# First halves' norms as steps inside the projection passes, a column-tiled sample memory attention, and the prompt's gates beside a pass

## What is computed

```python
for l in range(2):
    h_p, h_s = rmsnorm(y_p, norm_pre[l]), rmsnorm(y_s, norm_pre[l])
    mk_p, mv_p = mem_kv(mem_prompt, mem_norm[l], w_mem_kv[l])     # 256 memory tokens, 4 heads of 128
    mk_s, mv_s = cache_mem_k[l], cache_mem_v[l]                   # the samples' own, from a cache
    if l == 0:   # forgetting attention, 8 heads of 128
        q, k, v, lf, xq, gate = split_fox(h @ fox_w_in, fox_b_f)  # lf = log_sigmoid(f + b_f)
        mix_p = fox_prompt(q, k, v, lf)       # scores + cumsum(lf)_i - cumsum(lf)_j, causal softmax
        mix_s = fox_sample(...)               # against 2048 paged past keys and the new ones
    else:        # multi-scale causal pooling of u
        u, xq, gate = split_pool(h @ pool_w_in)
        mix = multiscale_pool(u, ...)
    y = y + rmsnorm(concat(mix, mem_attend(xq, mk, mv)) * silu(gate) @ w_out[l], norm_post[l])
```

## Time and profile before

| | |
|---|---|
| Three runs | 3638.39, 3642.01, 3642.56 us (median 3642.01) |
| Profiled execution | 3641.81 us, its span 3640.2 us |
| Mean granted clock of TensorE | 0.968 |
| Busy share: PE, PEld, DVE, ACT, POOL | 92%, 78%, 37%, 31%, 11% |
| DMA | 515.75 MB, mean 142 GB/s |

### The profile page before, as it was taken

One profiled execution on the slowest core, in us unless ns is written; L12 is line 12 of the kernel. 1 busy time (PEld: TensorE's weight loads), 2 busy tenths in 40 slices (PEclk: granted clock), 3 DMA queues, 4 the chain that ended last, 5 costly groups with the idle time before them and its releaser, 6 DMA issues. The chain is left out here.

```text
span 3640.2 us, 51875 instructions
## 1 busy us (share of the span) xinstructions
PE 3365.5 (92%) x19681; PEld 2844.2 (78%) x19681; DVE 1345.5 (37%) x2667; ACT 1133.0 (31%) x2210; POOL 397.2 (11%) x613
## 2 busy tenths in 40 slices
PE   5999899899999998959999998995999899996999
PEld 4999799777777766748888887884999778775887
DVE  3332313232222213535545554223222335565322
ACT  3122323122222223435556553112113344212211
POOL 1330000001111110112222220000000001121000
PEclk9999999999999999979999999997999999997999
DMA  3344333278889973332322305332332434565541
GB/s 117 115 149 137 123 95 119 79 227 281 275 290 294 291 226 116 124 107 79 92 80 88 102 27 189 110 98 68 111 118 94 130 100 135 178 189 179 164 122 52
DMA packets 409348, 515.75 MB, mean 142 GB/s; under 512 B 50791, under 2 KB 298088, under 8 KB 407551
## 3 DMA queue, kind: packets, MB, share of 16 engines
q1 hardware_dynamic: 386263, 444.74, 39.3%
q0 software_dynamic: 22848, 67.78, 5.8%
HBM read 388.57 MB, written 124.22 MB: 141 GB/s over the span
## 5 line engine op out<-in xcount | busy, mean ns | idle before, releaser
L459 ACT ACTIVATE z_st_p<-bank 128x352 f32<-128x352 f32 (+3 forms) x325 | 168.1, 518 | 786.6 <-PE bank L434 777.5
L1596 PE MATMUL bank<-w_hi_o,b_hi_o 128*128 128x512 f32 x816 | 319.5, 392 | 27.0 <-DVE w_lo_o L1655 27.0
L434 PE MATMUL bank<-h00hi,w_hi_p 128*128 128x352 f32 x984 | 323.4, 329 | 17.3 <-DVE w_lo_p L401 7.9
L1597 PE MATMUL bank<-w_hi_o,b_lo_o 128*128 128x512 f32 x816 | 318.9, 391 | 0.0
L1598 PE MATMUL bank<-w_lo_o,b_hi_o 128*128 128x512 f32 x816 | 318.9, 391 | 0.0
L434 PE MATMUL bank<-h00hi,w_lo_p 128*128 128x352 f32 x984 | 318.0, 323 | 0.0
L434 PE MATMUL bank<-h00lo,w_hi_p 128*128 128x352 f32 x984 | 317.8, 323 | 0.0
L434 PE MATMUL bank<-h01hi,w_hi_p 128*128 128x512 f32 x656 | 283.6, 432 | 13.8 <-DVE w_lo_p L401 11.5
L759 PE MATMUL bank<-pT_fa,v_fa 128*128 128x256 f32 (+1 forms) x1152 | 291.4, 373 | 1.7 <-DVE mix_fa L832 0.7
L399 DVE CAST w_hi_p<-w_raw_p 128x1024 fp32r<-128x1024 f32 (+1 forms) x130 | 92.6, 713 | 476.5 <-PE bank L434 418.7
L434 PE MATMUL bank<-h01hi,w_lo_p 128*128 128x512 f32 x656 | 259.3, 395 | 0.0
(11 more groups left out here) (318 smaller groups left out, 6966.3 us busy)
## 6 DMA issues: line engine op xcount, KB each, us to landing
k_raw_sf<-in_cache_fox_k SPq DMA_DIRECT2D x128, 512.0 KB, 4.6
v_raw_sf<-in_cache_fox_v POOLq DMA_DIRECT2D x128, 512.0 KB, 5.4
z<-z_st_p SPq DMA_DIRECT2D x112, 512.0 KB, 2.9
w_raw_p<-in_fox_w_in SPq DMA_DIRECT2D x80, 512.0 KB, 5.4
b_raw_o<-bT SPq DMA_DIRECT2D x32, 768.0 KB, 6.4
w_raw_p<-in_pool_w_in SPq DMA_DIRECT2D x48, 512.0 KB, 5.1
out<-tok_p SPq DMA_DIRECT2D x64, 256.0 KB, 3.2
w_raw_o<-in_w_out SPq DMA_DIRECT2D x24, 512.0 KB, 4.5
```

The source lines that it names most:

```text
L434: last = nc.tensor.matmul(bank[:, 0:width], wt[:, u, k, :], h[:, k, at0:at0 + width], start=(m == 0), stop=(m == MM - 1))
L459: nc.scalar.activation(z_st[0:rows_t, t % 2, at0:at0 + width], bank[0:rows_t, 0:width], tiles[t][2]).then_inc(z_read, 1)
L1596: nc.tensor.matmul(bank(t, half)[:, :], bh, w_hi[:, k, cols], start=(k == 0), stop=False)
L1597: nc.tensor.matmul(bank(t, half)[:, :], bl, w_hi[:, k, cols], start=False, stop=False)
```

## The change

- Constants become a `Work` beside p00, issued before anything else of it.
- `norm_transpose` is gone. `norm_rows` takes a list of tiles: the nine of the first half, a gap of two steps, the eight of the second. It is beside p00 and p10 with a plan that starts ahead of the pass (`EARLY`). Within a step, ScalarE and VectorE now do the copy and the subtraction of the tile before between the sum of squares and the root. TensorE waits ahead of each chunk of tile 0 for the rows that the chunk needs (3, 6, then 9 tiles of rows).
- The jobs of p00 and p10 begin with tiles 0 and 1 chunk by chunk: (0, chunk 0), (1, chunk 0), (0, chunk 1), and so on.
- The memory queries' tiles come first in both layers, ahead of the gate's.
- `memory_sample` works on fp32 keys, queries and values without `hi` and `lo` parts. Head h has the output partitions 32h to 32h+31. The normalisation moves from the probabilities to the output; scores, probabilities, products and output have two buffers each.
- `prompt_gates` becomes a `Work` of 14 steps beside p01 (tiles 33.3 to 40), in one PSUM bank, in four rounds for the sums.

In `project_pass` the first calls of `advance` below are SyncE's (GpSimd has the first too, ahead of the past gates' loads), the next ones VectorE's, and `ready` is TensorE's:

```diff
-    for t in range(NT):
+    FIRST = 2 if ready else 0
+    jobs = [(t, ch, None) for ch in range(C) for t in range(FIRST)]
+    for t in range(FIRST, NT):
         for ch in range(C):
             jobs.append((t, ch, None))
...
+            beside.advance(EARLY)
             load(0)
             load(1)
+            beside.advance(0)
...
+            beside.advance(EARLY / 2)
             split(0)
+            beside.advance(0)
+            for t in range(1, FIRST):
+                split(t)
...
                 if q == 0 and ch == 0:
                     pe.wait_ge(wlo_d, t + 1)
+                if q == 0 and t == 0 and ready:
+                    ready(pe, ch)
...
-                    norm = second_half(0, sems, sems, xp, hi1, lo1, [(28, 0), (len(tiles) - 1, 11)], ends_s)
+                    norm, normed = norms(0, sems, sems, xp, xs, (hi0, lo0), (hi1, lo1),
+                                         [(EARLY, 1), (EARLY / 2, 3), (0, 5), (0.6, 8), (1.2, 11), (28, 11), (len(tiles) - 1, 21)], ends_s)
...
-                        kv0, ends0 = prompt_rows(0, sems, room, [(0.5, 0), (9, 15)])
+                        kv0, ends0 = prompt_rows(0, sems, room, [(1.6, 0), (9, 15)])
...
+                        late = prompt_gates(nc, sems, room, const, banks[7], z0, F_ROW, fox_b_f, fox_lf_p, cT, [(33.3, 0), (40, 14)],
+                                            rows.when(XQ), ends_f)
...
-        tiles = (columns(D + XW + D, D + XW + D, XH, ACT.Silu) + columns(D, D, XH, ACT.Copy) + columns(0, 0, KT, ACT.Copy)
+        tiles = (columns(D, D, XH, ACT.Copy) + columns(D + XW + D, D + XW + D, XH, ACT.Silu) + columns(0, 0, KT, ACT.Copy)
```

`norm_rows`' streams for SyncE and ScalarE, and its tile order:

```diff
+    def tile(i, lag):
+        t = i - 1 - lag
+        t = t if t < hold else None if t < hold + GAP else t - GAP
+        return t if t is not None and 0 <= t < NT else None
...
+                if t >= 2:
                     sp.wait_ge(xn_d, t - 1)
+                sp.dma_start(x[0:rows, t % 2, :], src).then_inc(x_in[t % 2], 16)
...
+                nc.scalar.activation(xn[0:rows, u, :], x[0:rows, u, :], ACT.Square, accum_out=ss[0:rows, u:u + 1]).then_inc(sq_d, 1)
             t = tile(i, 1)
             if t is not None:
                 for j in range(2):
                     act.wait_ge(tr_d, 2 * t + j + 1)
+                    nc.scalar.copy(tiles[t][2][place(t, j)], turned(t, j)).then_inc(hi_d, 1)
+            t = tile(i, 0)
+            if t is not None:
+                u, rows = t % 2, tiles[t][1]
+                act.wait_ge(ms_d, t + 1)
+                nc.scalar.activation(ms[0:rows, u:u + 1], ms[0:rows, u:u + 1], ACT.Sqrt).then_inc(rt_d, 1)
```

`memory_sample` on TensorE, with SyncE's wait for a value buffer:

```diff
-                    sp.wait_ge(vl_d, b - 1)
+                    sp.wait_ge(pv_d, b - 1)
...
+                for t in range(NT):
+                    for h in range(XH):
+                        last = nc.tensor.matmul(O_BANK[b % 2][CT * h:CT * (h + 1), 0:P], pT[:, b % 2, t, CT * h:CT * (h + 1)],
+                                                v_raw[:, b % 2, t, h * P:(h + 1) * P], start=(t == 0), stop=(t == NT - 1))
+                last.then_inc(pv_d, 1)
...
+                for h in range(XH):
+                    last = nc.tensor.matmul(S_BANK[b % 2][CT * h:CT * (h + 1), :], qx[:, b, h, :], kT[:, b % 2, h, :], start=True, stop=True)
+                last.then_inc(s_done, 1)
```

More of the change, by code:

```diff
@@ L34 @@
 HIST = 15
+EARLY = -1.0
 class Core:
@@ L315, in slots, with opens @@
                     for q in range(Q):
-                        yield n, t, ch, part, q, t + (ch + (q + 1) / Q) / C
+                        yield n, t, ch, part, q, (done + (q + 1) / Q) / C
+                    done += 1
+        def opens(n, q):
+            t, ch, part = jobs[n]
+            if q != 1 or part is not None:
+                return None
+            if t < FIRST:
+                return FIRST if (t, ch) == (FIRST - 1, C - 1) else None
+            return t + 1 if ch == 0 and t + 1 < NT else None
         @block.sync
@@ L359, in _ @@
                     load(t + 2)
-                if ch == 1 and q == 1 and t >= 1:
+                if q == 1 and t >= 1 and ch == (C - 1 if t < FIRST else 1):
                     store(t - 1)
@@ new lines, in pe @@
+    def pe(pe):
+        for i in range(STEPS):
+            if i == 6:
+                pe.wait_ge(sub_d, 1)
+                for n in range(NQ):
+                    last = nc.tensor.transpose(bank[:, n * FH:(n + 1) * FH], fT[:, n * P:(n + 1) * P], ident[0:FH, 0:FH])
+                last.then_inc(tr_d, 1)
+            if ROUND0 <= i < ROUND0 + ROUNDS:
+                r = i - ROUND0
+                if r == 0:
+                    pe.wait_ge(scan_d, 5)
+                    pe.wait_ge(tri, 2)
+                else:
+                    pe.wait_ge(row_d, r)
+                for m in range(4):
+                    n = 4 * r + m
+                    out = bank[0:FH, m * P:(m + 1) * P]
+                    nc.tensor.matmul(out, lf[:, n, :], upto[:, :], start=True, stop=False)
+                    last = nc.tensor.matmul(out, pad[0][:, Z - 1 + n, :], ones[:, :], start=False, stop=True)
+                last.then_inc(ct_d, 1)
+            yield
@@ L996, in memory_rows, with norm_rows @@
     return Work(STEPS, plan, dict(sp=sp, pe=pe, act=act, dve=dve)), [(out, 16 * NT) for out in out_d]
-def norm_rows(nc, stack, room, tag, const, banks, rows, gain, hT_hi, hT_lo, plan, freed=()):
+def norm_rows(nc, stack, room, tag, const, banks, tiles, hold, gain, plan):
     ident = const["ident"]
-    NT = rows.shape[0] // P
+    NT = len(tiles)
     c = Core(nc, stack, tag, room)
@@ L1077, in pe @@
             if t is not None:
+                rows = tiles[t][1]
                 pe.wait_ge(xn_d, t + 1)
@@ L2416, in decoder_step @@
             o, F_ROW = 3 * D + FH, 3 * D + XW + BW
-            tiles = (columns(o + XW, 3 * D + XW, BW // P, ACT.Silu) + columns(o, 3 * D, XH, ACT.Copy)
+            tiles = (columns(o, 3 * D, XH, ACT.Copy) + columns(o + XW, 3 * D + XW, BW // P, ACT.Silu)
                      + [(3 * D, F_ROW, ACT.Copy, FH, None)]
```

586 lines of the change are left out of this document (223 added, 363 removed).

## The result

| | before | changed |
|---|---|---|
| Median (four runs each) | 3640.2 us (3636.2 to 3642.6) | 3508.9 us (3508.1 to 3509.9) |
| Ratio | | 0.9641, interval 0.9627 to 0.9656 |
| Span of the profiled execution | 3640.2 us | 3508.3 us |
| Mean granted clock | 0.968 | 0.978 |

The account below looks back on a forecast made before the run. TensorE, busy 3365.5 of 3640.2 us, was taken as the bound, so savings must be its work or idle time. Norms 41, gates 17 and sample memory 39.5 sum to 97.5: 3641.8 - 97.5 = 3544 us, range 3510 to 3590.

Parts of the forecast that it names:

- rival 4: SyncE becomes the bound: waits in the new sample memory attention delay the pass's weight loads; 3656 us; chance 0.04 with its like.
- Part B: Prompt's gates moved inside the second pass: 28.8 us saved ahead of attention, less work added to the pass; 17 us.
- Part A: First halves' norms moved into each layer's first pass: sixth evictions 21.4 and 19.8 us earlier; 41 us.
- The upper chain of the prediction: Upper estimate for nine tiles' norms, all waits in a row and matmuls before transposes: 6.7 us a tile, 60 us.
- the tail: From the norm chain's end to the sixth eviction in each layer: last chunks of two tiles, eviction, low clock; 10 us.
- The 2 us for a clock still low: Allowance after each layer's norm chain, before the sixth eviction, for TensorE's clock still at 1.2 GHz; 2 us.
- One sign: At the layers' starts, the wait for lo rows ahead of a chunk would be TensorE's largest; no size given.
- Part C: Sample memory attention with shorter steps, fewer waits and new tile order, in first and last pass; 39.5 us, bounds -10 and 54.
- of TensorE's 8.6 us of waits for evictions, 5: First pass: 5 us saved from TensorE's waits for evictions queued on ScalarE with the sample memory attention's copies.
- I leave 4 of stalls: Last pass: eight sample memory batches take 21 us plus 4 of stalls, so 26 us saved of at most 30.
- the Silu tiles under the prompt memory: Last pass: Silu tiles now beside the prompt memory's start add table loads, costing TensorE perhaps 5 us, at most 12.
- rival 2: All goes well: norm chains of 40 us, gates saving 20, sample memory 50; 3516 us; chance 0.12.

Follow-up runs that it names:

- e10: The changed kernel with the gain's load issued ahead of the first row load in each layer's norms; 3511.8 us.
- e8: The changed kernel with three row buffers instead of two in the norms inside the first passes; 3507.8 us.
- e13: The kernel before, with no step beside the pass taken in the whole chunk ahead of a tile's transposes; 3627.9 us, ratio 0.9971.
- e14: The kernel before, with the last pass's sample memory steps spread over 7.5 tiles instead of 5, prompt memory over 7; 3636.0 us, ratio 0.9995.
- e6: The changed kernel with two more ScalarE copies of 128 x 1024 in every sample memory step, written to an unread buffer; 3511.5 us.
- e1: The kernel before with the new sample memory routine alone; norms, gates and tile order unchanged; 3580.5 us, ratio 0.9835.
- e2: The kernel before with layer 1's tile order alone changed, copied columns ahead of Silu ones in the last pass; 3637.9 us, ratio 0.9997.
- e7: The changed kernel with the sample memory's score and value products issued twice; 3525.2 us.

## Why the prediction was right and wrong

**What bounds the kernel** was read rightly: TensorE's time and gaps paid for all of it, and SyncE never became the bound (rival 4).

**Part B** was right: 17 forecast, 17.5 alone. The 28.8 us came as read from the rows, the second pass grew by 9 to 11 where 12 were counted.

**Part A** had the right mechanism, and sizes on the dear side. (The upper chain of the prediction is added up wrongly: 6.0 and half of 1.9 are 7.0 a tile, 63 us and not 60. It didn't come to that.) In each layer: the first Square 1.6 us earlier, since the rows' load goes ahead of the gain's, and e10 shows that the place costs 1.8 us at the Square and 0.7 to 1.2 at the eviction; the chain 45.0 and 44.0 instead of 48 and 47, so the sharing counted at 3 us cost nothing over the kernel before's 44.7 (e8: it is loads that the chain waits for, and TensorE right behind them); the tail 8.2 instead of 10. The 2 us for a clock still low weren't there: the last evictions are 3.8 us apart. 6.4 us in each layer, 13 in all. One sign was wrong: TensorE's largest waits at the start of a layer are those of the norms' transposes for the scaled rows, 16.9 us in layer 0, and not those for the lo rows, 3.6.

**Part C** is the step that failed, in its terms for the waits and for the clock behind them.

- "of TensorE's 8.6 us of waits for evictions, 5", and in the last pass "I leave 4 of stalls": nothing of the last pass's 10.0 us was left, and of the first pass's 10.7 (8.6 at the transposes, 2.1 at the pass's matmuls) 0.9. The copies of turned tiles still hold it for 5.3 us there, 4.3 before. Why the rest went is in part argued: e13 and e14 show that the waits go when the old steps stand elsewhere, and e6 that a long ScalarE piece in the new step doesn't bring them back.
- The clock behind those waits, 5 us in the first pass and 7 in the last. In the first pass it was not in the sum. In the last it was, unnamed, since I took the old share from the stretch's length (51 us). It stood in the windows of the same stretches, which I had read for busy times. e13 and e14 take waits and clock away and leave the products: 11.7 us in the first pass and 13.4 in the last, where e1 has 18.5 with the old order of the tiles.
- Smaller, and beside the failed step: the new step is 2.3 us, not 2.6, and the old one 4.2 by the count, not 4.3. That is 14.5 us in the first pass where 13.5 were counted, and 2.2 less for the eight new batches of the last pass than the 21 taken. Values take 0.46 and scores 0.55 with the change of form in them; the 0.17 us for each change taken from the earlier trace rows was too much. The Trainium skill (TensorEngine Tiling (Array Packing), Key Properties) names a drain at such a change; whatever there is of it is inside these 2.3 us.
- For the Silu tiles under the prompt memory 5 us were counted. The last pass of the changed kernel is 2.7 us longer than e1's, which has the old order. Its trace has 2.3 us of wait for the load of the memory's keys and values there, which e1's hasn't, and 0.5 more for an exponential; the kernel before has 1.8 of the first with the old order too, so the order alone doesn't explain it, and its cause stays open. By e2 the table loads' place made no difference that can be measured.

By these: 14.5 + 9.8 + 5 = 29.3 for the first pass's 28.9, and 26 + 4 + 2.2 - 2.7 = 29.5 for the last one's 29.2. The ceiling was wrong as well: rival 2 allowed C 50 us and its upper bound was 54 (its own terms, 13.5 + 8.6 + 30, give 52), and the sample memory gave 58.5 alone. No rival had the clock behind the waits as a term.

## What to carry to other kernels

Read the granted clock in every window where the bounding engine has waits, and look at the slow stretch behind each wait: in the trace of the kernel before 21 us of waits carried 12 us of clock. It is no fixed rate, since e2 has the last pass's share of these waits with 2 us of clock in place of 7. Beside a bounding pass a step's cost is its time on that engine, plus what is due right behind it on the others' queues: look at the places, not at the sums of work. Moving steps away from those places (e13) gave 10.5 us without touching the step.

## What was not expected of the hardware

- 33 us of ScalarE copies beside TensorE's bound passes cost 2 to 3 us (e6); 13.8 us of added TensorE products cost 13 in the two passes that hold them, 16 in the kernel's time (e7).
- Twelve ACT_TABLE_LOADs of 1.28 us in 100 us did not make TensorE wait: with ten of them moved its waits there were 9.8 us instead of 10.0 (e2).
- The same waits came with a granted clock of 0.93 in one trace and 0.98 in another (before, e2).
- Eight value products of a 128x32 operand with 128 columns, fp32, take 0.46 us, 0.057 each, half of the 0.11 us of a product with 256 columns: here the time follows the columns down to 128.
